# A two-layer decoder trunk on one core: the expert stage and all before it run on halves of the tokens, woven unit by unit, instead of on all tokens one stage after another

## What is computed

```python
# layer 0 mixer: gated linear attention (4 heads) + stick-breaking attention (8 heads)
# layer 1 mixer: causal softmax attention (8 heads of 64; one block of 256 keys)
#                + a gated linear recurrence over the tokens (width 512)
x += mixer(rmsnorm(x)) @ w_out
x += cross_attention(rmsnorm(x), mem)      # 4 heads of 128, 256 memory tokens
x += peer_ffn(rmsnorm(x))

def peer_ffn(xi, wq, subkeys, u, v):       # for every token, 8 heads
    q = xi @ wq                            # 1024 -> 2048
    s = q . subkeys                        # 2 x 128 scores a head
    s1, i1 = top_k(s[0], 16); s2, i2 = top_k(s[1], 16)
    top_s, pos = top_k(s1[:, None] + s2[None, :], 16)
    eidx = i1 * 128 + i2 at pos            # 16 of 16384 experts a head
    g = softmax(top_s)
    act = gelu(xi . u[eidx])               # 128 dots of 1024 a token
    return sum((g * act) * v[eidx])        # 128 rows of 1024 a token
```

## Time and profile before

| | us |
|---|---|
| Median of 3 runs | 1933.07 (1929.70 to 1933.99) |
| Profiled execution, its own time | 1930.56 |
| Its span, first to last instruction | 1928.8 |
| PE busy | 1591.4 (83%) |
| VectorE busy | 1011.3 (52%) |
| ScalarE busy | 646.9 (34%) |
| GpSimd busy | 514.9 (27%) |
| DMA | 610.20 MB, 316 GB/s over the span |

### The profile page before, as it was taken

One profiled execution on the slowest core, in us unless ns is written; L12 is line 12 of the kernel. 1 busy time (PEld: TensorE's weight loads), 2 busy tenths in 40 slices (PEclk: granted clock), 3 DMA queues, 4 the chain that ended last, 5 costly groups with the idle time before them and its releaser, 6 DMA issues.

```text
span 1928.8 us, 15560 instructions
## 1 busy us (share of the span) xinstructions
PE 1591.4 (83%) x4638; PEld 806.3 (42%) x4638; DVE 1011.3 (52%) x2487; ACT 646.9 (34%) x1897; POOL 514.9 (27%) x516
## 2 busy tenths in 40 slices
PE   7999989767877877787779989997788777877876
PEld 4777778222322222222237666763232222222222
DVE  3432238688544554445441632489874445444454
ACT  1243221423433333333332433123343333333333
POOL 0000001434433433333300000015444343333331
PEclk9999999999999999999989999999999999999999
DMA  8321224999999999999933222359999999999996
GB/s 304 131 88 44 101 108 184 390 416 421 422 421 422 421 422 422 421 421 422 421 154 131 88 104 93 118 221 422 421 421 421 422 421 421 422 421 422 421 421 287
DMA packets 107540, 610.20 MB, mean 316 GB/s; under 512 B 10032, under 2 KB 10176, under 8 KB 41280
## 3 DMA queue, kind: packets, MB, share of 16 engines
q0 software_dynamic: 73728, 536.90, 67.1%
q1 hardware_dynamic: 33728, 72.30, 10.3%
HBM read 608.12 MB, written 1.05 MB: 316 GB/s over the span
## 4 chain that ended last, share of the span: by engine, by line
DMA 45%; PE 38%; DVE 9%; ACT 5%; issue 2%; POOL 0%; SPq 0%; DVEq 0%; PEldq 0%; ACTq 0%
DMA arena<-in_experts,idxT 45%; PE psum L516 37%; DVE arena L1416 5%; ACT cst L882 1%; ACT gains L882 1%; ACT arena L882 1%; ACT gelus L882 1%; ACT L882 1%; DVE red L1385 1%; DVE kv L1377 0%; POOL arena L1710 0%; DMA vecs<-in_vecs 0%; ACT sqb L882 0%; DVE kv L1383 0%; DVE red L1200 0%
## 5 line engine op out<-in xcount | busy, mean ns | idle before, releaser
L516 PE MATMUL psum<-arena,cst 128*128 128x512 f32 (+2 forms) x2112 | 1029.4, 616 | 283.6 <-ACT cst L882 279.1
L1416 DVE CUSTOM_DVE_ANT_0 arena<-arena,xrow 128x1024 f32<-128x1024 f32 x512 | 624.4, 1224 | 537.7 <-DMA arena<-in_experts,idxT 537.0
L1710 POOL DMA_INDIRECT arena<-in_experts,idxT x512 | 514.7, 1005 | 1387.8 <-PE psum L516 790.0
L516 PEld LDWEIGHTS psum<-arena,cst 128*128 128x128 f32 x2112 | 367.1, 191 | 942.5 <-ACT cst L882 645.7
L882 ACT ACTIVATE gelus<-red 128x1 f32<-128x1 f32 x512 | 103.6, 202 | 770.2 <-DVE red L1416 769.9
L516 PE MATMUL psum<-hT,ring 128*128 128x256 f32 x1280 | 293.3, 390 | 6.1 <-DVE hT L1215 6.1
L516 PEld LDWEIGHTS psum<-hT,ring 128*128 128x128 f32 x1280 | 248.9, 196 | 47.5 <-issue 9.8
L882 ACT ACTIVATE cst<-cst,gains 128x128 f32<-128x128 f32 x512 | 206.2, 403 | 23.2 <-PE psum L516 6.7
L882 ACT ACTIVATE gains<-gelus,gateT 128x1 f32<-128x1 f32 x512 | 150.8, 294 | 17.0 <-ACT gelus L882 0.2
L882 ACT ACTIVATE arena<-psum 128x512 f32<-128x512 f32 (+3 forms) x89 | 47.8, 545 | 304.3 <-PE psum L516 304.0
L516 PE MATMUL psum<-mixT,ring 128*128 128x256 f32 x256 | 57.4, 387 | 2.5 <-DVE mixT L1689 2.5
(11 more groups left out here) (161 smaller groups left out, 672.1 us busy)
## 6 DMA issues: line engine op xcount, KB each, us to landing
ring<-in_peer_wq SPq DMA_DIRECT2D x8, 2048.0 KB, 8.1
ring<-in_ev_w_in SPq DMA_DIRECT2D x6, 2048.0 KB, 11.8
ring<-in_od_w_in SPq DMA_DIRECT2D x5, 2048.0 KB, 33.0
ring<-in_xa_wkv SPq DMA_DIRECT2D x4, 2048.0 KB, 7.9
arena<-in_experts,idxT POOLq DMA_INDIRECT x512, 15.3
ring<-in_ev_w_out SPq DMA_DIRECT2D x2, 2048.0 KB, 7.8
ring<-in_xa_wq SPq DMA_DIRECT2D x2, 2048.0 KB, 9.2
ring<-in_xa_wo SPq DMA_DIRECT2D x2, 2048.0 KB, 7.7
```

The lines of the kernel that those rows point to most:

```text
L516: return nc.tensor.matmul(out, lhsT, rhs, start=start, stop=stop)
L1416: V.tensor_tensor_reduce(out=ut, in0=ut, in1=xrow[:, u // PAIRS, :], scale=1.0, scalar=0.0, op0=ALU.mult, op1=ALU.add, accum_out=dots[:, k ...
L1710: nc.gpsimd.indirect_dma_start(slot[slot_of(u)], None, d["experts"], bass.IndirectOffsetOnAxis(ap=idxT[:, u:u + 1], axis=0))\
```

## The change

It rewrites the order of the work in every engine's block, from the first cross attention on. The layer-0 mixer stays on all tokens. After it:

- `cross`, `peer` and the layer-1 mixer (`odd`) are done for one half t of 128 tokens at a time: every projection reads 128 columns (`quarters`: 4 x 8 matmuls of 128 columns into one bank) instead of 256. Softmax, recurrence and rotary work are done on halves; keys, values and the recurrence's state of half 0 are kept for half 1.
- The 512 units form four runs of 128, q = 2 * layer + half, without a break between them. All work of the stages is given a mark, a unit number at which it stands in the order: cross and routing of layer 0's half 1 lie in the units of half 0, layer 1's memory keys after them, layer 1's mixer, cross and routing of a half in the units of the run before.
- ScalarE and VectorE do their part of all units below a job's mark before the job; PE stays two units behind (`PE_LAG`).
- Weights are laid out by the host in blocks whose rows are contiguous 8 KB a partition, 1 MB (or 256 KB of subkeys) a block; the ring has 4 slots of 1 MB. From the first cross attention on, each weight but the memory's is loaded once for each half: 104 MB of blocks in all, 26 of them for layer 0 after its mixer and 54 for layer 1 without the memory's 4.
- 6 PSUM banks go round for jobs, 2 are kept for the sum of the units; the arena has 7 slots. A run of layer 1 begins its sum with the residual (8 transposes), and the output leaves in token order, without `back` at the end.
- ScalarE loads its tables by need (`table`): a unit wants the gelu's, a norm or a softmax the one with log and exp.
- Units can be summed on PE or VectorE (`ON_V`); `on_vector` returns False, so all 512 are PE's.

```diff
@@ constants
-BANKS = 8
+BANKS = 6
-BLOCK = 4096
+BLOCK = 2048
-SLOTS = 8
-UNITS = PAIRS * TT
+GATHERS = LAYERS * TT
+UNITS = GATHERS * PAIRS
+SLOTS = 7
+PE_LAG, SUM_LAG = 2, 3
...
+JOB_WEIGHT = {"pq": 8, "mq": 8, "mk": 8, "rx": 8, "rg": 8, "mv": 8, "xq": 8, "xo": 4, "od": 8, "xk": 8, "xv": 4}
+
+def spread(marks, jobs, first, last):
+    total = sum(JOB_WEIGHT.get(j[:2], 2) for j in jobs)
+    done = 0
+    for j in jobs:
+        marks[j] = first + (last - first) * done // total
+        done += JOB_WEIGHT.get(j[:2], 2)
+
+def route_marks(q, g):
+    if q == 0:
+        return ([0, 0, 0, 0, 0], [0, 0, 0, 0, 0], [0, 2, 4, 6, 8], [8, 10, 12, 14, 16])[g]
+    m = (0, 44, PAIRS + 84, 2 * PAIRS + 84)[q] + 10 * g
+    return [m, m + 3, m + 6, m + 7, m + 10]
+
+def unit_marks(jobs):
+    marks = {name: 0 for name in jobs}
+    spread(marks, cross_jobs(0, 1), 18, 42)
+    for q in range(1, GATHERS):
+        for name in peer_jobs(q // TT, q % TT):
+            marks[name] = route_marks(q, int(name[-1]) if "." in name else 0)[0]
+    spread(marks, KEY_JOBS, 88, 104)
+    for t in range(TT):
+        at = (t + 1) * PAIRS
+        spread(marks, [f"back{t}.0", f"back{t}.1"] + odd_jobs(t), at + 4, at + 60)
+        spread(marks, cross_jobs(1, t), at + 60, at + 82)
+    return marks
+
+def on_vector(u):
+    return False
@@ PE
             def job(name):
                 n = JOB[name]
...
+                units_to(UNIT_AT[name] - PE_LAG)
                 if n >= BANKS:
                     pe.wait_ge(psum_free[n % BANKS], n // BANKS)
...
+            def quarters(name, rhs, norm=None):
+                o, done = job(name)
+                for j in range(4):
+                    w = weights(f"{name}_{j // 2}")
+                    for k in range(KC):
+                        if norm and j == 0:
+                            pe.wait_ge(h_ready, KC * TILE_NORM[norm] + k + 1)
+                        last = mm(o[:, j * P:(j + 1) * P], w[:, k, j % 2 * P:(j % 2 + 1) * P], rhs[:, k, :],
+                                  k == 0, k == KC - 1)
+                last.then_inc(done, 1)
@@ ScalarE
+            def expert_unit(u):
+                q, k = divmod(u, PAIRS)
+                t, r, i = q % TT, u % 16, PE_COUNT[u]
+                table(GELU_TANH)
+                act.wait_ge(dotted, u + 1)
+                fn(gelus[:, r:r + 1], dots[:, k:k + 1], ACT.Gelu).then_inc(gelu_done, 1)
...
+            def take(name):
+                units_to(UNIT_AT[name])
+                return full(act, name)
@@ VectorE
+            def units_to(n):
+                while next_unit[0] < n:
+                    u = next_unit[0]
+                    expert_dot(u)
...
+                    if u >= PAIRS and u % PAIRS == SUM_LAG - 1:
+                        sum_up(u // PAIRS - 1)
+                    next_unit[0] += 1
@@ the order, the same on PE, ScalarE and VectorE
+            cross(0, 0)
+            peer(0, 0)
+            cross(0, 1)
+            peer(0, 1)
...
+            memory_keys()
+            for t in range(TT):
...
+                odd(t)
+                cross(1, t)
+                peer(1, t)
+            units_to(UNITS)
@@ GpSimd
-            for l in range(LAYERS):
-                for u in range(UNITS):
...
+            for u in range(UNITS):
+                q, k = divmod(u, PAIRS)
+                if k % 32 == 0:
+                    pool.wait_ge(idx_ready, 4 * q + k // 32 + 1)
+                if u >= SLOTS:
+                    taken(pool, u - SLOTS)
```

More of the change, by code:

```diff
@@ L110, in weight_blocks, with add @@
 def weight_blocks(d):
-    def cols(w, at, n=512):
-        return w[:, at:at + n].rearrange("(k p) n -> p k n", p=P)
     out = []
+    def add(name, src, last):
+        out.append((name, src, last))
     def keys(l):
[L119 to L128, removed]
@@ L139, in weight_blocks, with values, cross @@
-    keys(1)
-    out += [(f"od_out{b}", cols(d["od_w_out"], 512 * b), f"od_out{2 * b + 1}") for b in range(2)]
-    rest(1)
+        for i in range(2):
+            add(f"xk{l}_{i}", d[f"xa_wkv{l}"][i], f"xk{l}.{i}")
+    def values(l):
+        for i in range(2):
+            add(f"xv{l}_{i}", d[f"xa_wkv{l}"][2 + i], f"xv{l}.1")
+    def cross(l, t):
+        for i in range(2):
+            add(f"xq{l}{t}_{i}", d[f"xa_wq{l}"][i], f"xq{l}{t}")
+        for i in range(2):
+            add(f"xo{l}{t}_{i}", d[f"xa_wo{l}"][i], f"xo{l}{t}.{i}")
@@ L204, in psum_jobs @@
-    jobs.extend(f"rgate{i}" for i in range(4))
-    attention("ms", "mt", "mm", MO_H, 2, MO_LAG, {KEY_STEPS[0]: ["xk1.0"], KEY_STEPS[2]: ["xk1.1"]})
-    jobs.extend(["xkn1.0", "xkn1.1"])
-    projection("od_out", "xa1", ["xv1.0"])
-    cross(1)
-    peer(1)
-    return {name: n for n, name in enumerate(jobs)}
+    fill = {KEY_STEPS[0]: ["glan0", "glan1", "xk0.0"], KEY_STEPS[2]: ["xk0.1"]}
+    for h in range(SB_H + SB_LAG + 1):
+        if h < SB_H:
+            jobs.append(f"sbz{h}")
+        if 0 <= h - SB_LAG < SB_H:
+            jobs.append(f"sbr{h - SB_LAG}")
+        if h - SB_LAG - 1 >= 0 and (h - SB_LAG - 1) % 2 == 0:
+            jobs.append(f"sbo{(h - SB_LAG - 1) // 2}")
+        jobs.extend(fill.get(h, []))
@@ L805, in _ @@
+            for i in range(2):
+                rows(f"xv0.{i}", ["xv0_0", "xv0_1"], hT, i)
             pe.wait_ge(gla_out, 1)
             copied(pe, *parts("sbo", 4))
[L807 to L817 removed]
@@ new lines, in _ @@
+            for i in range(4):
+                name = f"ev_out{i}"
+                o = full(dve, name)
+                x2 = xT[:, 2 * i:2 * i + 2, :]
+                V.tensor_tensor(x2, x2, pairs(o), ALU.add).then_inc(bank_free(name), 1)
+            cross(0, 0)
+            peer(0, 0)
+            cross(0, 1)
+            peer(0, 1)
+            memory(1, memT)
+            memory_keys()
+            for t in range(TT):
+                for b in range(2):
+                    residual(f"back{t}.{b}", b, t)
+                odd(t)
+                cross(1, t)
+                peer(1, t)
```

1757 lines of the change are left out of this document (887 added, 870 removed).

## The result

| | us |
|---|---|
| Changed kernel, median of 9 runs | 1939.24 (1934.58 to 1951.11) |
| Kernel before, median of 9 runs on the same chip | 1931.58 (1929.06 to 1933.99) |
| Ratio | 1.0045, 95% interval 1.0024 to 1.0067 |
| Profiled execution of the changed kernel, its span | 1946.37, 1944.6 |

What follows compares the result with a forecast made beforehand. DMA at 421 GB/s was taken as the bound: floor 1740 us, plus start-up 13, layer 0 losses 13, layer-1 losses 2 x 19, end 9.5, gave 1813.5 of span, 1815 profiled, 1818 us median; range 1765 to 1890.

Steps and rivals of the forecast that it cites:

- rival 3: Half-width matmuls don't get cheaper, 75 us more PE a layer-1 run, about 1905 us in all; chance 6%.
- Run 3 and the end: Last run of 128 units, nothing woven in: 319 us; last dot to the end: 9.5 us.
- None on VectorE: Summing of units: leaving none to VectorE costs zero, since PE already sums all 512.
- PE's cost of a half: A layer-1 half's projections, norms, scores and the like: 120 us of PE woven into 128 units of 1.71 us.
- Floor: 286 + 1275 + 179: Whole kernel: 286 us to first gather, 1275 of gathers, 179 of weights beside them at 421 GB/s, 1740.
- Nothing, while routing keeps to its marks: ... 26 us, under 30 of DMA: Second start-up gone at no loss: ten units and 13 us of routing on VectorE fit beside the DMA.
- Loss 12 us a run: Layer 1's mixer, 56 units: tight around the softmax heads on ScalarE, costing 12 us a run (0 to 40).
- arena slots 7 for 8 ... nothing (up to 5): Gather slots: one fewer costs nothing (up to 5 us), as five gathers in flight last 12 us.
- Borders of a run, 3 us within the slack: Between runs: residual transposes, `back` once a half and copying out a sum, 3 us each, hidden by the slots.
- Cross attention, 7 us a run: Cross attention, 22 units: 72 us with PE's short waits against 65, a loss of 7 a run (0 to 20).
- rival 4: Woven jobs stop units on all three engines and gathers stop once seven slots fill: 2006 us, slower; chance 5%.
- Rival 2: Dependent hops of softmax and norm bound the layer-1 runs, 30 hops at 3 us exposed: about 1880 us; chance 22%.

Runs made afterwards that it cites:

- the fillers: Changed kernel with one or two zero-adding PE matmuls per unit in layer 1's mixer and cross attention: 2014.43 and 2117.83 us.
- The early scores: Changed kernel with PE's and ScalarE's projection and scores of the routing's second to fourth groups five units earlier: 1908.36 us.
- the routing's own lag: Changed kernel with PE four units behind, not two, only for the routing's norm, projection and scores: 1913.34 us.
- Lags, leads and wider marks: Changed kernel with PE four units behind everywhere, 1941.22 us; VectorE three units ahead, 1934.24; eight slots, earlier scores and woven work spread over more units, 1871.10.
- the best version: Changed kernel with eight gather slots, earlier routing scores and woven work spread over more units: 1871.10 us, ratio 0.9687 to the kernel before.
- Run 0: Not a follow-up: the changed kernel's first 128 units (layer 0, half 0) with start-up; forecast 390 us, measured 424.4.
- the cures: Eight gather slots, earlier routing scores and woven work spread over more units, together on the changed kernel: 1871.10 us.
- run 2: Not a follow-up: the changed kernel's third 128 units (layer 1, half 0), with woven work; forecast 405 us, measured 457.7.
- run 1: Not a follow-up: the changed kernel's second 128 units (layer 0, half 1), with woven work; forecast 405 us, measured 446.7.

## Why the prediction was wrong, point by point

**Right.** The first gather came at 287.6 (286). A projection on 128 columns costs half: 64 instructions in 7.31 us, 0.114 each, so rival 3 is dead. 536.90 MB of gathers and 652 in all (640 forecast). Run 3 and the end. "None on VectorE" prices at nothing. The total in full slices stayed at 421 GB/s. The Trainium skill, DMA: Bandwidth & Descriptors, has 425 GB/s for large transfers of a core whose pair is idle (section Bandwidth) beside the 358 of its Specifications; the trace sides with the first.

**PE's cost of a half: right in size.** Counted were 159 us in the mixer's 56 units and 60 in cross attention. Measured are 173.0 and 59.1 busy, at a clock of 0.94 and 0.92; 173 times 0.94 is 163. The clock was not in the sum. It fell from 0.99 in the gather stretches to 0.93 in the woven ones, and the fillers show that raising it by added work does not pay.

**Wrong: the frame of the sum.** "Floor: 286 + 1275 + 179" takes the DMA as what is full, with losses on top. That held before, whose gathers had nothing beside them that stopped PE. In the woven runs the DMA is idle for 7 to 13% of the time, and 194 us of its bytes weigh 14. The run of a woven half is set by the ring: by the hops of its jobs plus the units between them, with only the slots to decouple the two.

**Wrong: "Nothing, while routing keeps to its marks: ... 26 us, under 30 of DMA".** This is the largest single step. I added VectorE's own work and left out its wait for the projection and scores, which PE begins only at VectorE's mark, in the same place of the order. The 127 us that I had priced for units 82 to 123 became 151.8 and 155.5. A group took 35 us, and in front of the first one two units took 24.7, 20 more than the DMA needs for them, through the norm. In sum 25 and 29 us a run. The earlier trace rows showed 42 of 50 us busy with the DMA full, and I read them as proof; but PE's 73 instructions in that window are the units' alone, since there the projections had been done beforehand. The early scores gave back 31 us, the routing's own lag 26.

**Wrong: "Loss 12 us a run" for the mixer.** Measured 18 and 25 over the price, so a loss of 30 and 37, inside the 0 to 40 that I had given it but far from its middle. I compared each engine's sum with the DMA's, 36 of ScalarE against 25. I take it that what counts is their sum in sequence, since conv, scan and heads pass from one to the other; no run shows this by itself. At the softmax heads POOL stood still for 9.67 us at 1345.95, and the DMA's share in 1340 to 1350 was 0.34:

```profile
1340.00:1350.00 10.00, 8.10 (x29) 4.44 (x30) 5.43 (x10) 4.64 (x16) 1.88 (x2) 0.66 0.34 116
```

Of this I found no cure. Lags, leads and wider marks left it between 3.4 and 3.9 us a unit against 3.1 of DMA (174 in 56), and the best version still has 3.56.

**Wrong: "arena slots 7 for 8 ... nothing (up to 5)".** 19 us for the eighth slot, 67 for the seventh. I counted the gathers in flight against the DMA's latency. They have to outlast the time in which PE frees no slot. In the three woven runs POOL stood for 9 us or more 23 times, mostly for up to 10.9, and for 15.7 to 17.1 at the first group of each routing, against the 15 that six gathers last when all of them are in flight.

**Small terms.** Borders of a run, 3 us within the slack: 6 us at each of the first two, exposed, PE waiting 5.6 for the sum to be copied out; at the third PE waited 5.0 and the units lost nothing. Cross attention, 7 us a run: 65 for 72, better than priced. Run 0 lost 34, almost all between units 16 and 83, in the cross attention and routing of the second half, by the same waits.

**Rivals.** The kernel came out slower than before, which I had given 5% (rival 4). What came is the mechanism of rival 4 (the units stop on all three engines, the slots fill) at the size of 34 to 53 us a run beyond my own loss, just under the 55 from which I had said it decides. Rival 2's dependent hops are its other half, but not in the place where I had put them: routing lost as much as softmax and norms. I gave the two 27% and priced them apart, each with the slots as a buffer that is full when the wait comes. They share one buffer.

**Open.** Together the cures gave back 68 of the 121 us between 1818 and 1939. Shown by edits are the slots and the place of the routing's scores. That the rest, the mixers above all, is lost in the same way is argued from the traces. Why mixer and routing of run 2 are 7 and 4 us slower than those of run 1 was not told apart. That the first group's chain of 20 us could be moved ahead too was not tried.

## What to carry to other kernels

When stages are woven over in-order queues that form a ring through a few buffers, don't compare each engine's sum with the bound. Walk one job through all queues at its place in the order, add what each engine stands still, and compare the longest stop with what the buffers last. Put the producer's part of a job several units ahead of its consumer's mark, and spend memory on another slot before trimming work: here these two gave 58 us, more than halving PE's unit work (4, at a lower clock), dropping 82 MB (14) or removing the table loads (14).

## What the runs showed of the hardware

- The TensorE clock fell when work was taken away, though PE stayed at work in small pieces. In the last run, with two instead of four instructions a unit every 2.49 us, the granted clock was 0.64 for 0.99, and PE's busy time 233 us for 254. So nearly half of the unit work was gone and PE was busy almost as long: the stretch was a mix of 2.4 and 1.2 GHz, where it had been at 2.4 nearly throughout. Behind a wait of 6.39 us a unit's four instructions took 3.78 us for 1.98.
- 82 MB more or less beside 537 MB of gathers moved the time by 14 us, though the DMA share was 0.91: a share of 0.9 over a long stretch did not make the DMA the bound.
- One float32 projection of 64 instructions of 128 columns took PE 7.31 us, 0.114 each, where 256 columns had 0.218.
- A table load of ScalarE took 1.28 us, and the instruction behind it began 0.01 us later.
